# Delta mixer: head sums by a full block of ones, roots by logarithm, unsplit empty units, and copies from the middle of the last tile

## The reference

```python
def l2norm(x):
    return x * lax.rsqrt(jnp.sum(x * x, axis=-1, keepdims=True) + EPS)

z = h @ w_in
qkv, gate, a_logit, b_logit, cfm_in = jnp.split(z, [s1, s2, s3, s4], axis=-1)
qkv = jax.nn.silu(causal_dwconv(qkv, gdn_conv_w)).astype(jnp.float32)
q, k, v = jnp.split(qkv, 3, axis=-1)
q = l2norm(q.reshape(shp))
k = l2norm(k.reshape(shp))
...
L = jnp.where(strict, jnp.einsum('nbhid,nbhjd->nbhij', kb, kc) * decay, 0.0)
sol = lax.linalg.triangular_solve(eye + L, rhs, left_side=True, lower=True, unit_diagonal=True)
```

## Time and profile before

| | us |
|---|---|
| median of 3 runs | 2194.64 |
| lowest to highest | 2194.15 to 2194.77 |
| the profiled execution, its own time | 2198.1 |
| its span, first to last instruction | 2196.3 |
| PE busy in the span | 2062.6 (94%) |
| PE weight load | 1691.0 (77%) |
| DVE, ACT, POOL busy | 979.5 (45%), 932.0 (42%), 935.5 (43%) |

### The profile page before, as it was taken

The page is one execution under the profiler, slowest core; times in us unless marked ns, Lnnn a source line. Parts: engine busy times, 40 slices in busy tenths (PEclk is TensorE's granted clock), DMA queues, the critical chain, the costliest instruction groups (busy, mean ns, idle before and its releaser), DMA issues.

```text
span 2196.3 us, 27648 instructions
## 1 busy us (share of the span) xinstructions
PE 2062.6 (94%) x9842; PEld 1691.0 (77%) x9842; DVE 979.5 (45%) x1103; ACT 932.0 (42%) x1112; POOL 935.5 (43%) x424
## 2 busy tenths in 40 slices
PE   2999989999999999899999999988999959999996
PEld 2788867787878787788888887878888747888885
DVE  6155541454545455411113347767672374333213
ACT  2366662232323332434333266566653325555321
POOL 3422213443424234344444447678255243444441
PEclk9999999999999999999999999999999979999998
DMA  7211103524243322232333322200233112332331
GB/s 273 88 57 58 58 20 107 186 72 162 87 147 109 135 86 90 70 99 95 95 100 93 107 84 77 67 30 1 99 114 125 43 54 78 94 95 95 106 105 48
DMA packets 56232, 203.69 MB, mean 93 GB/s; under 512 B 6240, under 2 KB 6368, under 8 KB 55904
## 3 DMA queue, kind: packets, MB, share of 16 engines
q1 hardware_dynamic: 56160, 202.70, 28.2%
HBM read 200.57 MB, written 2.10 MB: 92 GB/s over the span
## 4 chain that ended last, share of the span: by engine, by line
PE 80%; DVE 10%; ACT 5%; issue 2%; POOL 2%; DMA 1%; DVEq 0%; ACTq 0%; SPq 0%; POOLq 0%
PE acc L1797 20%; PE acc L1799 20%; PE acc L1798 20%; PE aux L1797 2%; PE aux L1799 2%; PE aux L1798 2%; ACT sp L527 2%; PE acc L2006 2%; DVE cfy L1427 1%; PE aux L2225 1%; PE aux L1920 1%; DMA ada<-in_ada 1%; POOL w_lo L469 1%; PE aux L1861 1%; PE aux L1854 1%
## 5 line engine op out<-in xcount | busy, mean ns | idle before, releaser
L469 POOL TENSOR_TENSOR w_lo<-raw,w_hi 128x1024 fp32r<-128x1024 f32 x324 | 797.1, 2464 | 1152.0 <-ACT w_hi L527 1151.0
L1797 PE MATMUL acc<-x_hi,w_hi 128*128 128x512 f32 x1512 | 602.3, 398 | 14.0 <-DVEq L1041 6.0
L1798 PE MATMUL acc<-x_lo,w_hi 128*128 128x512 f32 x1512 | 592.1, 392 | 0.0
L1799 PE MATMUL acc<-x_hi,w_lo 128*128 128x512 f32 x1512 | 591.6, 391 | 0.0
L527 ACT ACTIVATE w_hi<-raw 128x1024 fp32r<-128x1024 f32 x324 | 342.8, 1060 | 533.2 <-PE acc L1799 408.6
L1797 PEld LDWEIGHTS acc<-x_hi,w_hi 128*128 128x128 f32 x1512 | 286.1, 189 | 86.7 <-DVEq L1041 11.6
L1799 PEld LDWEIGHTS acc<-x_hi,w_lo 128*128 128x128 f32 x1512 | 285.7, 189 | 60.8
L1798 PEld LDWEIGHTS acc<-x_lo,w_hi 128*128 128x128 f32 x1512 | 286.1, 189 | 57.3 <-issue 0.2
L527 ACT ACT_TABLE_LOAD x85 | 109.1, 1283 | 44.7 <-DVE tn L1756 20.8
L1756 DVE SCALAR_TENSOR_TENSOR tn<-acc,cols,tn 128x511 f32<-128x511 f32 x88 | 65.9, 749 | 121.3 <-ACT tn L527 114.9
L1072 DVE SCALAR_TENSOR_TENSOR adac<-ada,c_act,adac 128x1024 f32<-128x1024 f32 x42 | 65.7, 1565 | 98.2 <-DMA ada<-in_ada 97.3
(11 more groups left out here) (427 smaller groups left out, 3237.3 us busy)
## 6 DMA issues: line engine op xcount, KB each, us to landing
raw<-in_weights SPq DMA_DIRECT2D x324, 512.0 KB, 3.5
ada<-in_ada SPq DMA_DIRECT2D x48, 512.0 KB, 3.7
resid<-in_x SPq DMA_DIRECT2D x1, 2048.0 KB, 12.8
out<-resid SPq DMA_DIRECT2D x8, 256.0 KB, 2.0
decay<-in_tables SPq DMA_DIRECT2D x4, 256.0 KB, 3.6
memf<-in_mem SPq DMA_DIRECT2D x1, 1024.0 KB, 4.8
angles<-in_tables SPq DMA_DIRECT2D x1, 512.0 KB, 3.4
small<-in_small SPq DMA_DIRECT2D x1, 320.0 KB, 3.2
```

The costliest lines, as they stand in the source:

```text
L469: nc.gpsimd.tensor_tensor(w_lo[s][:], raw[s][:], w_hi[s][:].bitcast(F32), ALU.subtract).then_inc(lo_ready, 1)
L1797: M(out, a_hi, b_hi, start=first, stop=False)
L1798: M(out, a_hi, b_lo, start=False, stop=False)
L1799: return M(out, a_lo, b_hi, start=False, stop=last)
```

## The change

1. **Head sums by ones.** For each head one matmul with the full block of ones as stationary operand and the squares as moving operand (`head_sums(h, bk)`) leaves the sum, spread over all partitions, in an `aux` bank: banks 0 to 3 for k ahead of tile 14, banks 0, 1, 4, 5 for q. The 16 one-column matmuls, the `spread` matmuls (`head_spread`) and the two reciprocals go. Each sum waits for its own square.
2. **Roots by logarithm.** ACT takes Ln of the sums with eps as bias and then Exp of -0.5 times it, in place in PSUM: once 2048 wide for k, twice 1024 wide for q (after the SiLU of gate tiles 0 and 1). Each begins with a preload of the table set that holds both functions. DVE's product of k moves into `conv_tile(5)`, ahead of its wait for ACT's tap.
3. **Empty units.** ACT and POOL pass units 25 to 27 by raising `hi_ready` and `lo_ready`, without copy and subtraction.
4. **Order on PE.** Tile 21 comes ahead of the transposes of v's last two chunks, and all four turns of `xt` come just before tile 24.
5. **Copies.** Tile 24 raises `x_half` after its fourth slice; ACT's copies to `xm` wait for that and stand ahead of gate tile 3's SiLU. `gate_tile(3)` waits for `unit_used` as the other gate tiles do.

```diff
@@ POOL
             for j in range(28):
-                split_lo(At(U0["gdn_in"] + j))
+                if j < 25:
+                    split_lo(At(U0["gdn_in"] + j))
+                else:
+                    pool.wait_ge(hi_ready, U0["gdn_in"] + j + 1)
+                    pool.sem_inc(lo_ready, 1)
@@ ACT
                 s = u.slot(RING)
                 act.wait_ge(raw_loaded[s], (u.div(RING).val() + 1) * 16)
+                if u.i is None and U0["gdn_in"] + 25 <= u.c < U0["gdn_in"] + 28:
+                    act.wait_ge(unit_used, (u + (1 - RING)).val())
+                    nc.scalar.sem_inc(hi_ready, 1)
+                    return
...
-            def roots_of_heads():
-                own["gstat_done"].next()
-                own["groot_ready"].own(f(rcol[:, 0:16], aux[:, 5 * T:5 * T + 16], ACT.Sqrt, bias=eps[:, 0:1]))
+            def roots_of_heads(first, n):
+
+                own["gstat_done"].next(n)
+                sums = aux[:, first * T:(first + n) * T]
+                nc.scalar.preload_act_table_set("natural_log_exp_and_others")
+                roots(sums, 1.0, sums, own["groot_ready"])
...
                 if k == GDN_H:
-                    roots_of_heads()
+                    roots_of_heads(0, GDN_H)
             for n in range(GDN_H):
                 split_hi(g0 + GATE + n + AHEAD)
+                if n == GDN_H - 1:
+                    act.wait_ge(S["x_half"], 1)
+                    for c in range(NB):
+                        own["x_turned"].next()
+                        own["x_first"].own(f(xm[:, c, :], aux[:, c * T:(c + 1) * T]))
                 own["logits_ready"].next()
                 step.own(f(sgate[:, n, :], sgate[:, n, :], ACT.Silu))
                 cfm_taps(EARLY_POOL)
-                if n == 0:
-                    roots_of_heads()
-
-            for c in range(NB):
-                own["x_turned"].next()
-                act.wait_ge(unit_used, U0["gdn_in"] + 28)
-                own["x_first"].own(f(xm[:, c, :], aux[:, c * T:(c + 1) * T]))
+                if n < 2:
+                    roots_of_heads(4 * n, 2)
@@ DVE
                 own["scaled"].own(V.tensor_tensor(bank(t), bank(t), rs_sb, ALU.mult))
                 cfm_taps(1)
+                if between:
+                    between()
                 own["tap_made"].next()
...
             conv_tile(4)
-            inverse_of_roots()
-            conv_tile(5)
-            own["hs_ready"].next()
-            own["k_normed"].own(V.tensor_tensor(flat(kf), flat(kf), aux[:, 0:4 * T], ALU.mult))
+
+            def norm_k():
+                own["groot_ready"].next()
+                own["k_normed"].own(V.tensor_tensor(flat(kf), flat(kf), aux[:, 0:4 * T], ALU.mult))
+
+            conv_tile(5, norm_k)
...
             def gate_tile(n):
-                dve.wait_ge(unit_used, U0["gdn_in"] + GATE + n + 1 if n < GDN_H - 1 else U0["gdn_in"] + 28)
+                dve.wait_ge(unit_used, U0["gdn_in"] + GATE + n + 1)
@@ PE
-            own["gsq_ready"].next(GDN_H)
-            head_sums(5 * T, kdec).then_inc(S["gstat_done"], 1)
+            pe.wait_ge(S["dec_ready"], NB)
+            for h in range(GDN_H):
+                head_sums(h, h)
             gdn_tile(14)
-            own["hrecip_ready"].next()
-            pe.wait_ge(S["dec_ready"], NB)
-            head_spread(range(4), 0)
             gdn_tile(15)
...
             gdn_tile(19)
             gdn_tile(20)
+            gdn_tile(21)
             own["xt_ready"].next(2)
             to_tokens(vf, 2, 4)
             to_tokens(vf, 3, 5)
-            turn(0)
-            turn(1)
-            gdn_tile(21)
-            own["kv_token"].next(4)
-            own["gsq_ready"].next(GDN_H)
-            head_sums(5 * T, kdec).then_inc(S["gstat_done"], 1)
+            head_sums(0, 0)
+            head_sums(1, 1)
+            own["kv_token"].next(2)
             to_tokens(kf, 0, 2)
             to_tokens(kf, 1, 3)
             gdn_tile(22)
...
+            head_sums(2, 4)
+            head_sums(3, 5)
             own["kv_token"].next(2)
             to_tokens(kf, 2, 2)
             to_tokens(kf, 3, 3)
             gdn_tile(23)
+            own["kv_token"].next(2)
             own["q_normed"].next()
-            head_spread((2, 3), 4)
-            own["kv_token"].next(2)
+            turn(0)
+            turn(1)
             turn(2)
             turn(3)
-            gdn_tile(24, extra=3)
```

36 lines of the change are left out of this document (18 added, 18 removed).

## The result

| | before | after |
|---|---|---|
| median, same chip | 2194.39 us (2194.15 to 2194.77) | 2181.86 us (2180.36 to 2182.03) |
| profiled execution, its own time | 2198.1 | 2181.72 |
| its span | 2196.3 | 2179.8 |

The ratio is 0.9941, with a 95% interval of 0.9928 to 0.9954: **12.5 us faster (0.6%)**, where 21.7 were forecast (2172.9). The time lies above the upper end of the range, 2179.0. Measured a second time, the medians were 2182.45 and 2196.33, a gain of 13.9 us.

What follows compares the result with a forecast made beforehand. PE was taken to bound the kernel (80% of the chain, DVE 10%). Loop start 19.3 us earlier plus 2.4 makes 21.7: 2198.1 to 2176.4, less 3.5 to the median, 2172.9 us; range 2170 to 2179.0.

Steps and rivals of the forecast that it cites:

- Head sums and tile 14: First head sums of k: no wait for three squares, tile 14 at full clock; tile 15 starts 10.0 us earlier.
- Roots: k's roots on ACT in conv_tile(5): DVE waits 1.3 us there, then 2.2 in conv_tile(6).
- rival B: ACT late at the roots, each table switch costing as much again as its load: 3.5 us lost, 2176.4; chance 0.06.
- The rest of DVE's work is unchanged, 20.05 us busy: DVE up to conv_tile(8): same busy time as before, so conv_tile(8) starts 7.8 us earlier.
- Rival D: DVE gains more: a 2.58 us mask product in lower(0) falls clear of POOL, 1.9 us less, 2171.0; chance 0.08.
- rival A: PE's clock falls in the 2 us gap before tile 21: 1.7 us lost, 2174.6; chance 0.18.
- Tile 21's order: Tile 21 ahead of the turns starts at 1403.6 instead of 1417.1: 13.5 us, of which 5.7 from the order.
- Empty units at nothing: Three splits fewer on ACT and POOL before the loop: alone they give nothing.
- Copies from half: Copies to xm from the middle of tile 24: the 3.7 us wait goes, full clock gives another 2.4.
- In the loop, DVE and PE take turns as before: Solving loop after the first xm update: no change in its 62 us.
- the loop's growth: Sign of being wrong: if the loop's 62 us (1458.7 to 1521) grow, ACT or POOL paces it.
- Beyond, everything hangs on these engines: Behind the loop: the 21.7 us gained by the first xm update carry through to the end.

Runs made afterwards that it cites:

- five taps moved: The changed kernel with five of DVE's convolution taps moved from conv_tile(7) to (10) and behind lower(1) to where DVE idles: 2178.64 us, again 2180.65.
- empties split: The changed kernel with units 25 to 27 copied and subtracted again on ACT and POOL: 2185.89 us.

## Why the prediction was wrong, by its own steps

Two terms of the sum were mis-sized: DVE's work up to conv_tile(8), 2.4 us, and the loop, 1.8 us. A third part, 3.0 us behind the loop, is the clock's, and the forecast had nothing for it. Step by step:

- **Head sums and tile 14**: right. No wait for `kdec`; the next tile follows 3.03 us later (3.5 were forecast) and runs at 1.00.
- **Roots**: right. Load 1.28, Ln 1.94, Exp 1.86; DVE waits 1.41 (1.3) and then 2.02 (2.2). Ln begins 0.01 us behind the end of the load, and the load 0.03 behind SiLU. The drain of 1.38 us that the Trainium skill has (ScalarE: Activation LUTs, "What ACT_TABLE_LOAD costs") is not in this trace, and rival B falls with it. (With 1.38 for 1.28 in rival B's own terms that drain would have come to 3.9 us, not to the 3.7 of the forecast, an estimate from that page.)
- **"The rest of DVE's work is unchanged, 20.05 us busy"**: wrong, and the term that was mis-sized in B. A duration read beside one neighbour was carried to another moment: 0.75 became 1.14 in conv_tile(6) and 2.79 in conv_tile(7), 2.4 us together. conv_tile(8) was 5.4 us earlier, not 7.8, and tile 21 began 56.3 us behind tile 13's end instead of 54.0. The kernel with five taps moved agrees: without them there B is 87.2. Rival D hoped for the opposite, a mask product clear of POOL; that product took 2.55 us again.
- **Gap before tile 21, rival A**: the gap of 1.9 us came ahead of v's first transposes, and the clock fell behind it (0.66). That cost nothing, which was luck: PE still came to tile 21 0.3 us before DVE had freed its bank. In the kernel with empties split the clock stayed up there and fell behind a wait of 1.9 us ahead of tile 21 instead; that cost 1.7 us, rival A's price.
- **Tile 21's order**: nearly right. Tile 21 started 67.1 us behind tile 13's end before and starts at 56.3 now; 5.4 of the 10.8 us are conv_tile(8)'s, 5.4 the order's and the turns' (5.7 forecast). By the first update the order alone is worth 2.3.
- **Empty units at nothing**: wrong in the new order, 2.5. This is not part of what is missing, since the forecast's sum had no wait there and the change, without these splits, has none. I had seen that the last one comes "about level" with tile 24's last eighth, and yet costed as if it came in time without the change.
- **Copies from half**: the wait goes, the loop starts 86.1 us behind tile 13's end (84.1 forecast), and 4.4 us later comes the first update instead of 3.2, its tap being 1.56 beside POOL. But the signal at half holds 1.7 of it.
- **"In the loop, DVE and PE take turns as before"**: wrong by 1.8, by the same rule of 0.55 us. I had named the loop's growth as the sign of ACT or POOL pacing it; it was POOL, but through DVE's own instructions.
- **"Beyond, everything hangs on these engines"**: wrong in what it left out. D was 3.0 us longer here, and undelayed kernels have 674.6 to 680.5, mostly by when the clock falls at the same two waits. The range needed that width, and so did the step from the profiled execution to the median: 3.5 us were taken off as a constant, while 2.8 of the difference between the two profiles lay ahead of tile 13.

In numbers: of 21.7 us 3.2 are missing in B, 1.8 in C and 3.0 in D; A gave 2.8 that nobody had counted on. That is the 16.5 between the spans. The medians have 12.5, because before's profiled execution stood 3.7 above its median and the changed kernel's 0.1 below. The 3.2 are counted from a B of 109.0 before; three other profiles of it have 110.1 to 110.2, so that part of the gain is 18.5 to 19.7.

## What to carry to other kernels

The length of an instruction that shares something with a neighbour is not a property of the instruction: when a change shifts two engines against each other, read for each of the shifted ones what ran beside it, and price it at both lengths. A late engine whose lateness was covered costs nothing to mend until the cover is removed; price such edits in the new order, not the old. And where runs spread by more than the effect, compare distances inside the profile: between two places 90 us apart the variants of the changed kernel repeated to 0.1 us, where two medians of one of them lay 4.3 apart (2190.2 and 2185.9). Look at the granted clock inside the distance before you give the difference to the edit: it held 1.6 us in the kernel before and 1.7 in the one with empties split.

## What the runs showed of the hardware

- A DVE tap with both tensor operands in SBUF that begins while POOL works ends 0.55 us after POOL's current instruction (43 of 45), so a tap of 0.75 us takes up to 2.8 beside a split of 2.4. A DVE product with one operand in PSUM takes 0.70 beside the same.
- With POOL's additions cut to one column the loop took 54.2 instead of 63.6 us, and DVE was busy for 42.7 of them instead of 54.4.
- After the same 2.5 us of idle time PE's clock fell at once in some executions, and in others stayed at 1.00 (first place) or fell some 2.4 us later (second place). It differed by when the idle time came; what sets it no run shows. In executions of one kernel on one chip the times lay up to 8.7 us apart (2192.15 to 2200.84) with the same code.
